# A two-block transformer on one core: the power's result becomes the norm factor, and key factors are turned from the small tile

## What is computed

```python
def _rms(x, w=None):                     # and rmsnorm, the same
    y = xf * lax.rsqrt(jnp.mean(xf * xf, axis=-1, keepdims=True) + EPS)
def l2norm(x):
    return x * lax.rsqrt(jnp.sum(x * x, -1, keepdims=True) + EPS)
# differential attention: q and k are normed by head and half head (width 64),
# scores are scaled by 1/8; its output is normed again (nt below)
s = jnp.einsum('bhrqd,bhrkd->bhrqk', qn, kn) * scale
# gated delta rule: q normed and scaled by 128 ** -0.5; output normed (no)
# mLSTM: hout = num / maximum(abs(den), exp(-mt)); output normed (nml)
# block 1's final norm (nfin) is followed at once by layer 0's norm (na)
```

## Time and profile before

| | before |
|---|---|
| median of 3 runs | 3216.72 us (3214.06 to 3218.84) |
| the profiled execution, device time | 3220.86 us |
| its span, first to last instruction | 3219.1 us |
| mean granted TensorE clock | 0.986 |
| PE busy | 3152.5 us, 98% |
| DVE, ACT, POOL busy | 34%, 39%, 54% |

### The profile page before, as it was taken

The page is one execution under the profiler, slowest core; times in us unless marked ns, Lnnn a source line. Parts: engine busy times, 40 slices in busy tenths (PEclk is TensorE's granted clock), DMA queues, the critical chain, the costliest instruction groups (busy, mean ns, idle before and its releaser), DMA issues.

```text
span 3219.1 us, 41315 instructions
## 1 busy us (share of the span) xinstructions
PE 3152.5 (98%) x15522; PEld 2570.1 (80%) x15522; DVE 1110.5 (34%) x2242; ACT 1251.7 (39%) x2260; POOL 1739.5 (54%) x1355
## 2 busy tenths in 40 slices
PE   9999999999999999999999999999999999999999
PEld 8888877787777788788888878877888777788887
DVE  5322322123555533223222565523111349321124
ACT  4333333224444435333223432335333446543334
POOL 5555664555555466456555523247555653565564
PEclk9999999999999999999999999999999999999999
DMA  5333322332222234233333211112333321233332
GB/s 165 98 99 92 92 83 75 89 92 72 66 66 69 66 100 117 79 92 99 98 98 95 77 43 51 49 59 83 98 95 98 95 82 40 76 92 96 98 105 82
DMA packets 149844, 275.42 MB, mean 86 GB/s; under 512 B 16528, under 2 KB 17808, under 8 KB 149520
## 3 DMA queue, kind: packets, MB, share of 16 engines
q1 hardware_dynamic: 149648, 272.79, 29.0%
HBM read 270.63 MB, written 2.10 MB: 85 GB/s over the span
## 4 chain that ended last, share of the span: by engine, by line
PE 92%; DVE 4%; issue 1%; ACT 1%; POOL 1%; DMA 0%; DVEq 0%; ACTq 0%; POOLq 0%
PE PS L753 90%; PE PS L821 2%; DVE TMP L1383 0%; ACT TMP L2169 0%; DVE AR L1383 0%; DVE PS L1383 0%; DVE AR L1389 0%; DVE ACC L1383 0%; DVE PS L2129 0%; POOL SM L2557 0%; POOL WL L2557 0%; DVE HL L1389 0%; DVE X L1389 0%; DVE ACC L1389 0%; POOL TMP L2557 0%
## 5 line engine op out<-in xcount | busy, mean ns | idle before, releaser
L2557 POOL TENSOR_TENSOR WL<-RAW,WH 128x512 fp32r<-128x512 f32 x1002 | 1301.4, 1311 | 902.3 <-ACT WH L2169 901.2
L2169 ACT ACTIVATE WH<-RAW 128x512 fp32r<-128x512 f32 x1002 | 620.8, 629 | 1040.0 <-PE PS L753 984.8
L753 PE MATMUL PS<-HH,WH 128*128 128x512 f32 x2264 | 899.3, 397 | 6.6 <-DVE HL L1389 3.2
L753 PE MATMUL PS<-HL,WH 128*128 128x512 f32 x2264 | 887.6, 392 | 1.3 <-DVE HL L1389 1.3
L753 PE MATMUL PS<-HH,WL 128*128 128x512 f32 x2264 | 887.2, 392 | 0.0
L753 PE MATMUL PS<-AH,WH 128*128 128x512 f32 (+1 forms) x1504 | 585.7, 389 | 7.2 <-ACT AH L2169 4.4
L753 PE MATMUL PS<-AL,WH 128*128 128x512 f32 (+1 forms) x1504 | 582.8, 388 | 2.2 <-POOL AL L2557 1.1
L753 PE MATMUL PS<-AH,WL 128*128 128x512 f32 (+1 forms) x1504 | 582.5, 387 | 1.0 <-POOL WL L2557 1.0
L753 PEld LDWEIGHTS PS<-HH,WH 128*128 128x128 f32 x2264 | 428.7, 189 | 99.9 <-issue 11.1
L753 PEld LDWEIGHTS PS<-HL,WH 128*128 128x128 f32 x2264 | 428.6, 189 | 91.1 <-DVE HL L1389 3.7
L753 PEld LDWEIGHTS PS<-HH,WL 128*128 128x128 f32 x2264 | 428.3, 189 | 90.7
(11 more groups left out here) (228 smaller groups left out, 2542.4 us busy)
## 6 DMA issues: line engine op xcount, KB each, us to landing
RAW<-in_wst SPq DMA_DIRECT2D x1002, 256.0 KB, 2.6
X<-in_x SPq DMA_DIRECT2D x8, 256.0 KB, 5.4
TMP<-in_p SPq DMA_DIRECT2D x8, 256.0 KB, 3.1
out<-X SPq DMA_DIRECT2D x8, 256.0 KB, 2.0
AR<-in_dm SPq DMA_DIRECT2D x1, 1024.0 KB, 6.7
AR<-in_mem SPq DMA_DIRECT2D x1, 1024.0 KB, 5.7
CST<-in_cst SPq DMA_DIRECT2D x1, 740.0 KB, 7.1
AR<-in_pos SPq DMA_DIRECT2D x2, 256.0 KB, 2.9
```

The costliest lines, as they stand in the source:

```text
L753: return e.matmul(o, l, r, start=a, stop=z, skip_group_check=True)
L2169: return e.activation(o, a, f, **kw)
L2557: return e.tensor_tensor(o, a, b, op)
```

## The change

- The Newton step is gone. POOL's power writes the factor itself; `nr(n)` is part 1 of the tile, and the steps ("x", n) are taken out of the plan. Each variance is written once.
- A scale in front of a norm enters through the epsilon: `x*pre*rsqrt(m*pre^2 + EPS)` equals `x*rsqrt(m + EPS/pre^2)`. `scaled_variance` is one instruction with a ready tile `eps`. That tile takes one instruction for nfin/na and for nt (in place of a reciprocal), two for nml (in place of a reciprocal), and for nq it is the variance itself, so POOL's four powers of the q norms go.
- Constant scales (1/8, 1/16) enter as factors of 64 and 256 on the variance; nd's variance is two instructions.
- The steps ("d_wide", h) are gone. "d_n" reads the small tile, and for each token quarter it issues one transpose of 128x64 to partitions 0 to 63 and one plain fp32 matmul with the identity to partitions 64 to 127. It waits for POOL's power instead of for the wide tile.
- The bank of a norm's sums is lent until the variance is read (label "var"), no longer until the factor is done.
- LATE keeps its offsets, but the steps that they count are fewer (some 60 lines of the lists differ by removed "x" and "d_wide" entries alone). By `turns`, POOL's part of ("mq", 5) now stands before POOL's part of ("d_t1", 7); DVE's part of ("l", 0, 2, 2) stands after ("m_q", 1) and that of ("l", 1, 2, 2) after ("l", 0, 3, 1); DVE's part of ("fin", 2) stands before ("zf", 3).

```diff
@@ the end of DIFF
-    ("d_pv", 7), ("mq", 4), ("d_t1", 7), ("x", ("nt", 7)), ("mq", 5), ("d_t2", 7),
+    ("d_pv", 7), ("mq", 4), ("d_t1", 7), ("mq", 5), ("d_t2", 7),
@@ names
         def nr(n):
-            return nwt(n, 2)
+            return nwt(n, 1)
@@ PE
                 elif kind == "d_n":
                     h = i[0]
-                    e.wait_ge(*at("d_wide", h))
-                    turned(("d_normed", h), ("d_n", h), lambda t: quarter(tmp(3), t))
+                    e.wait_ge(*at("factor", ("nd", h)))
+                    r = nr(("nd", h))
+                    o = bank("d_normed", h)
+                    for t in range(4):
+                        e.transpose(quarter(o, t)[0:64], r[:, t, 2:3].to_broadcast([128, 64]), ident)
+                        z = mm(quarter(o, t)[64:128], r[:, t, 3:4].to_broadcast([128, 64]), ident, True, True)
+                    z.then_inc(*up("mm", "d_n", h))
...
-                    o = bank("factor", n)
+                    o = bank("var", n)
@@ DVE
             def variance(n, done=None):
 
                 mult = NORM[n][1]
+                if n[0] in ("nr", "nk", "nd") and n[1] > 1:
+                    e.wait_ge(*at("factor", (n[0], n[1] - 2)))
                 e.wait_ge(*at("mm", *(done or ("fac", n))))
-                ts(nwt(n, 0), held(n, 0), mult, EPS, MUL, ADD).then_inc(*up("var", n))
-                ts(held(n, 1), held(n, 0), mult, EPS, MUL, ADD).then_inc(*up("var_held", n))
...
+                if n[0] == "nd":
+                    ts(nwt(n, 0)[:, :, 0:2], sums(n)[:, :, 0:2], 64.0 * mult, 64.0 * EPS, MUL, ADD)
+                    ts(nwt(n, 0)[:, :, 2:4], sums(n)[:, :, 2:4], mult, EPS, MUL, ADD).then_inc(*up("var", n))
+                elif n == "nqm":
+                    ts(nwt(n, 0), sums(n), 256.0 * mult, 256.0 * EPS, MUL, ADD).then_inc(*up("var", n))
+                elif n[0] == "nq":
+                    ts(nq_eps(n[1]), sums(n), 128.0 * EPS * mult, 128.0 * EPS * EPS, MUL, ADD).then_inc(*up("var", n))
+                else:
+                    ts(nwt(n, 0), sums(n), mult, EPS, MUL, ADD).then_inc(*up("var", n))
+
+            def scaled_variance(n, eps):
+
+                post = NORM[n][5]
+                if n[0] in ("nt", "no", "nml") and n[1] > 1:
+                    e.wait_ge(*at("factor", (n[0], n[1] - 2)))
                 e.wait_ge(*at("mm", "fac", n))
-                stt(held(n, 2), held(n, 0), mult, pre, MUL, MUL).then_inc(*up("var_once", n))
-                e.wait_ge(*at("var_once", n))
-                tt(held(n, 2), held(n, 2), pre, MUL).then_inc(*up("var_twice", n))
-                e.wait_ge(*at("var_twice", n))
-                ts(nwt(n, 0), held(n, 2), EPS, None, ADD).then_inc(*up("var", n))
-                ts(held(n, 1), held(n, 2), EPS, None, ADD).then_inc(*up("var_held", n))
+                stt(nwt(n, 0), sums(n), NORM[n][1] / post ** 2, eps, MUL, ADD).then_inc(*up("var", n))
...
-            def factor(n, pre=None):
...
-                e.wait_ge(*at("root", n))
...
-                tt(held(n, 2), held(n, 1), nwt(n, 1), MUL).then_inc(*up("root_once", n))
-                stt(held(n, 2), held(n, 2), -0.5 * post, nwt(n, 1), MUL, MUL).then_inc(*up("root_error", n))
...
-                    stt(nr(n), held(n, 2), 1.5 * post, nwt(n, 1), ADD, MUL).then_inc(*up("factor", n))
...
-                    tt(nr(n), held(n, 1), pre, MUL).then_inc(*up("factor", n))
...
-                elif kind == "d_wide":
...
-                    src = held(("nd", h), 1)[:, :, 2:4].unsqueeze(3).to_broadcast([128, 4, 2, 64])
-                    e.tensor_copy(tmp(3).rearrange("p (a b c) -> p a b c", a=4, b=2), src).then_inc(*up("d_wide", h))
-                    ts(eighth(h), held(("nd", h), 1)[:, :, 0:2], 0.125, None, MUL).then_inc(*up("d_eighth", h))
...
                 elif kind == "d_t1":
-                    e.reciprocal(d_once(h), d_stats(h)[:, :, 4:5]).then_inc(*up("d_once", h))
...
-                    scaled_variance(("nt", h), d_once(h))
+                    n, den = ("nt", h), d_stats(h)[:, :, 4:5]
+                    stt(nwt(n, 2), den, EPS / NORM[n][5] ** 2, den, MUL, MUL).then_inc(*up("den_eps", h))
...
+                    scaled_variance(n, nwt(n, 2))
@@ POOL
-                tt(w[:, 1, :], w[:, 0, :], neghalf.to_broadcast([128, nc_]), POW).then_inc(*up("root", n))
+                tt(w[:, 1, :], w[:, 0, :], neghalf.to_broadcast([128, nc_]), POW).then_inc(*up("factor", n))
-                elif kind in ("r_fac", "d_f", "d_t1", "fk", "fq", "zf", "m_f"):
+                elif kind in ("r_fac", "d_f", "d_t1", "fk", "zf", "m_f"):
```

More of the change, by code:

```diff
@@ L367, in split @@
         h = i[0] if i else None
[L368 to L373, removed]
+        if kind == "d_v":
+            out += [s, ("d_f", h)]
         elif kind == "d_q" and i[1] == 0:
@@ L421 @@
-    ("d_rope", 3, 1), ("d_add", 3, 1), ("r_out", 3, 5), ("d_sc", 3, 0), ("d_t1", 2), ("x", ("nt", 2)), ("d_sc", 3, 1), ("d_q", 4, 0),
+    ("d_t1", 1), ("d_q", 3, 0), ("d_gain", 3), ("d_sm", 2, 0), ("d_turn", 2, 0), ("d_sc", 2, 2), ("d_t2", 1), ("d_sm", 2, 1),
+    ("d_q", 3, 1), ("d_sc", 2, 3), ("d_turn", 2, 1), ("d_sm", 2, 2), ("d_v", 3), ("d_f", 3), ("d_vt", 3), ("r_out", 3, 4),
+    ("d_turn", 2, 2), ("d_sm", 2, 3), ("g", 0, 5), ("d_turn", 2, 3), ("d_n", 3), ("d_pv", 2), ("d_rope", 3, 0), ("d_add", 3, 0),
@@ L994, in tensor @@
                         if m == 2:
-                            opened["nqm"] = bank("factor", "nqm")
+                            opened["nqm"] = bank("var", "nqm")
                         p = m // 2 - 1
@@ L1214, in tensor @@
                     h = i[0]
-                    o = bank("factor", ("no", h))
+                    o = bank("var", ("no", h))
                     e.wait_ge(*at("d_out_square", h))
@@ L1389, in stt, with sums @@
                 return e.scalar_tensor_tensor(out=o, in0=a, scalar=s, in1=b, op0=op0, op1=op1)
-            def held(n, a):
+            def sums(n):
                 _, _, _, nt, nc_, _ = NORM[n]
-                return (psum("d_eighth", n[1]) if n[0] == "nd" else psum("factor", n))[:, 0:64 * nt].rearrange("p (t c) -> p t c", t=nt)[:, :, a * nc_:a * nc_ + nc_]
+                return psum("var", n)[:, 0:64 * nt].rearrange("p (t c) -> p t c", t=nt)[:, :, 0:nc_]
             def variance(n, done=None):
@@ L1755, in vector @@
                     e.wait_ge(*at("ms_max", h, q))
-                    e.wait_ge(*at("mem_scale"))
-                    ts(st[:, 1:2], st[:, 0:1], mem_scale[:, q, h:h + 1], -1.0, MUL, MUL).then_inc(*up("ms_neg", h, q))
+                    e.wait_ge(*at("factor", "nqm"))
+                    ts(st[:, 1:2], st[:, 0:1], nr("nqm")[:, q, h:h + 1], -1.0, MUL, MUL).then_inc(*up("ms_neg", h, q))
                 elif kind == "mx":
@@ L2350, in scalar @@
                         e.wait_ge(*at("mem_lo", 7))
-                    act(mem_p(q), psum("ms_exp", h, q)[:, 0:256], ACT.Exp, st[:, 1:2], mem_scale[:, q, h:h + 1], st[:, 2:3]).then_inc(*up("ms_exp", h, q))
+                    act(mem_p(q), psum("ms_exp", h, q)[:, 0:256], ACT.Exp, st[:, 1:2], nr("nqm")[:, q, h:h + 1], st[:, 2:3]).then_inc(*up("ms_exp", h, q))
                 elif kind == "mt":
```

135 lines of the change are left out of this document (49 added, 86 removed), and 28 rows, old and new, of tables (AB, MEM, SWA).

## The result

The changed kernel takes 3227.87 us (median of 9 runs, 3223.68 to 3228.70), the kernel before 3216.72 (9 runs, 3214.06 to 3223.28): a ratio of 1.0034, 95% interval 1.0025 to 1.0043. It is 11 us slower, by about a third of a per cent; the forecast was 3219.6, with "slower" at 0.22.

A forecast was written before the change was run, and what follows sets the result against it. PE was taken to bound the kernel, 92% of the chain. Gains of 7.2 us against costs of 10.05 gave +2.85, set on the median of 3216.72: 3219.6 us, range 3209 to 3229.

The forecast's parts named there:

- rival B: Transposes and plain matmuls on PE drain each other: d_n +14.8 us, total +11.9, 3228.6; 0.22 including in-between cases.
- Item 4: d_n on PE, eight times: 1.16 us in place of 0.43, +0.73 a head, +5.8 in all; bounds +2.3 and +14.8.
- Item 5: POOL's order at head 7: mq 5's addition ahead of nt's power, a new 4.0 us stall, 1.1 back: +2.9.
- Item 6: DVE's order in the delta rule: row 2's last update behind m_q 1, a new PE stall of 1.15 us.
- Item 7: Head 3's output norm: ("fin", 2) now ahead of its variance on DVE, cost 0.2 us.
- Item 1: mLSTM norms of heads 0, 1 and 2: shorter PE stalls, gain 1.2 us each, 3.6 together.
- Item 2: nmem's norm: its 1.44 us PE stall goes, gain 1.4; the other plain factor gains 0.5.
- Item 3: DVE's queue relieved: gain 1.0 us at d_turn of head 1 and 0.7 at a q norm.
- Item 8: Granted clock: -1.5 us for one slow stretch gone cancels a new one behind the 4.0 us stall; zero net.

The follow-up runs named there:

- experiment 3: Changed kernel with d_n's four transposes first and its plain matmuls behind them, one change of kind in place of seven: 3221.90 us in one run.
- experiment 2: Changed kernel with d_n as plain fp32 matmuls for both column halves, no transposes: 3218.58 us in one run.
- experiment 4: Changed kernel with d_n's transposes and plain matmuls alternating in full 128x128 form into the same quarter, first half's factor left out: 3219.00 us in one run.
- experiment 5: Changed kernel with d_n's plain matmul on the same lower half as the transpose, upper half unwritten: 3228.80 us in one run.
- experiment 6: Changed kernel with one LATE offset changed, mq 5 from -1 to -0.4, to put POOL's order at head 7 back: 3217.67 us in one run.
- experiment 7: Changed kernel with the step lists and LATE of the kernel before, removed steps standing empty, so every engine has its old order: 3217.49 us (10 runs).
- experiment 10: Changed kernel with d_n as 128x128 transposes after DVE's copy from the small tile, LATE reset to the old order, no empty steps: 3203.38 us (5 runs).
- experiment 1: Kernel before with only the changed kernel's d_n, read from the small tile, and DVE's wide copy left out: 3232.88 us (4 runs), ratio 1.0059.

## Why the prediction was right where it was, and wrong where it was

The time lay in the range (3209 to 3229), 8 us above the forecast, in the outcome to which I gave 0.22. That it meets rival B's 3228.6 within a microsecond is in part luck: d_n alone cost more than B had, and a cover that I did not count took it back.

- **Item 4 is the step that failed, by the size of its term.** I took d_n at 1.16 us, "the transposes hide beside" the plain matmuls, from a row in which records of one kind alternate. Measured: 2.33. The sum had +5.8, it should have had +15.2. That is above even the upper bound of 14.8, which had ten changes at 0.1 and twelve records at 0.107: in experiment 3 each change that is saved is worth 0.13, and the twelve records with one change take 1.54. The row that I took was right for what it showed (0.064 a record in experiment 2, 0.126 within a half in experiment 3); what was missing was a row in which the two kinds meet on column halves, and I had said so under rival B. Such a gap should have weighed more than the one row that was near. Rival B was the truth, in its place, its price and its point of decision (1.6 us a head), but only on column halves: in the full form the two kinds follow each other without a loss (experiment 4). Whether what costs is a drain, as B says, no run shows.
- The rule that I set against B was that only a change of the tiling mode and not of the tile drains TensorE (the Trainium skill, TensorEngine Tiling (Array Packing), Key Properties). It speaks of tiles and not of kinds. For tiles experiment 2 agrees with it: sixteen records that alternate between the two halves take 0.064 us each. But within one form, 128*64, and even on one and the same half, each change between transpose and plain matmul costs (experiment 5), so the rule was no argument against B. The Trainium skill says on the same page, under Restrictions, that column tiling disables the transpose mode for fp32 input. Experiments 4 and 5 agree with it in so far as something about transposes is other on column halves; what, no run here shows. The transposes on halves still stand as one record each, where a plain fp32 matmul has two.
- Item 5: 3.76 us, predicted 4.0 (I took POOL's addition at 1.26 where its row has 1.30, which changes nothing); the stall of 1.09 behind it gone, as predicted; the slow stretch behind it came, as predicted.
- Item 6: 1.20, predicted 1.15. Item 7: 2.80 in place of 2.45, predicted +0.2. Three places at which a removed step moved another one were read off the list before any run, and experiments 6, 7 and 10 confirm them.
- Item 1: the stalls 1.95, 1.52 and 1.50 fell to 0.73, 0.30 and 0.50, by 1.22, 1.22 and 1.00; predicted 1.2 each.
- Item 2: nmem's stall fell from 1.44 only to 1.05, not to nothing. PE came there sooner, because its slow stretch was gone (0.80 against 1.00 in the windows). The gain is there, as clock. The other plain factor's half microsecond is gone.
- Item 3: d_turn's 0.98 is gone. At the q norm DVE's queue was not relieved as I thought: where 1.33 stood PE now waits 1.60, with small stalls ahead of it rearranged. Its 0.7 did not come.
- A cover that I did not count: three stalls of 1.24 us for ACT behind d_n, which the longer d_n fills (2.9 us). It works against the error of item 4, and it comes back as soon as d_n is short.
- Item 8: I set the clock to zero. Both profiles of the changed kernel miss less clock, by 6.4 and 9.6 us, but the average over all runs has it 1 us less, near the zero that I took. With item 4 at +15.2 and everything else as predicted (+4.25 order, -7.2 gains), the sum would be +12.3; the medians differ by 11.2. The gains that did not come in items 2 and 3, and a stall of 1.03 at the delta rule's gates that no item has (last section), are by their size what the cover of 2.9 and that microsecond of clock take back.

## What to carry to other kernels

Where a row is used to price an instruction sequence, look whether it holds the same mixture of kinds, not only the same shape: here plain matmuls on halves and transposes in the full form each had a row, and the price was in their alternation on halves. When steps are taken out of a list whose offsets count steps, compare the order of every engine before and after; three such shifts cost this kernel 5.5 us of stalls, where the Newton steps gave 7.3. And a copy that is hidden on an idle engine is cheaper than one that is saved by work on the engine that bounds. Last, compare the clock over all runs and not over two profiles: a slow stretch can hide a stall, and its absence can show one, as the last section has it.

## What the runs showed of the hardware

- A transpose next to a plain fp32 matmul costs nothing in the full 128x128 form (0.11 from start to start, experiment 4), but on column halves it is 0.20 to 0.23 from the transpose to the plain matmul and 0.36 from there to the next transpose, 0.59 for a quarter where the full form takes 0.33. The half doesn't matter (experiment 5), the number of changes does (experiment 3). The mechanism stays open.
- A DVE tensor_tensor can be held by POOL. Two of 128x32 in the gates of the delta rule took 0.42 us in the kernel before, with POOL idle, and in the changed kernel 1.45 beside a POOL instruction that began at 1836.12 and lasted 1.27:

```profile
1823.25 0.42 DVE L1383 TENSOR_TENSOR Z<-Z 128x32 f32<-128x32 f32 x2
...
1836.21 1.45 DVE L1373 TENSOR_TENSOR Z<-Z 128x32 f32<-128x32 f32 x2
...
1836.12 1.27 POOL L2516 TENSOR_TENSOR WL<-RAW,WH 128x512 fp32r<-128x512 f32 x1 [0.56 <-ACT WH L2128]
```

  All fourteen traces agree: 0.42 in the three with the Newton steps (the kernel before twice, experiment 1), 1.44 to 1.48 in the eleven others. Why it is held no run shows. So when work shifts by a few microseconds, which DVE instruction falls beside which of POOL's shifts too.
- A slow stretch of PE can hide a wait. Behind these gates PE needs DVE's result, and how long it stands still depends on two things, the hold and PE's own granted clock in the 4 us before. That clock is at its upper level, 1.00, or at its lower one, 0.50, and PE's matmuls there follow each other by 0.12 or 0.21 us. Without the hold it waits nothing at a clock of 0.50 (the kernel before, both profiles) and 2.19 at 1.00 (experiment 1). With the hold it waits 0.88 to 1.25 at 0.50 (the changed kernel's first profile, experiments 3 and 6) and 3.10 to 3.25 at 1.00 (the eight others). The hold costs about 1.0 at either level, and the upper level turns slow matmuls into idle time. Experiment 1, then the first and the second profile of the changed kernel, each with a window (columns of the earlier trace rows):

```profile
1839.62 0.59 PE L753 MATMUL PS<-SC,CST 128*128 128x16 f32 x4 [2.19 <-DVE SC L1391]
1837.00:1841.00 4.00, 1.81 (x12) 1.50 (x11) 2.41 (x17) 2.85 (x5) 1.38 (x2) 1.00 0.15 53
...
1840.68 0.58 PE L738 MATMUL PS<-SC,CST 128*128 128x16 f32 x2 [1.03 <-DVE SC L1376]
1837.00:1841.00 4.00, 2.97 (x14) 2.70 (x14) 3.22 (x18) 1.32 (x4) 0.65 (x2) 0.50 0.38 119
...
1840.47 0.59 PE L738 MATMUL PS<-SC,CST 128*128 128x16 f32 x4 [3.23 <-DVE SC L1376]
1837.00:1841.00 4.00, 0.77 (x7) 0.59 (x7) 3.01 (x18) 2.85 (x5) 0.65 (x2) 1.00 0.35 115
```

  So a stall that is new in one profile need not cost time: it has to be read together with the clock in front of it.
